# Turning heads, probabilities and gates in 32x32 squares on VectorE, with the squares moved by DMAs within SBUF

## The reference

```python
h = rms_norm(x, norm_w, 1e-6);  proj = h @ w_in        # q_a k/v_c k/v_s k/v_w gates z_a q_b k_b v_b z_b
# group A: 8 heads of 128, 2 kv groups: compressed, selected and window branch, sigmoid gate per head and branch
o_a = g0 * o_cmp + g1 * o_sel + g2 * o_win
# group B: 4 heads with two softmax maps, a = p[:, 0] - lam * p[:, 1]; o = rms_norm(a @ v) * (1 - lambda_init)
mixed = concat([o_a * silu(z_a), o_b * silu(z_b)])
x = x + mixed @ w_out;  return rms_norm(x, final_norm_w, 1e-6)
```

## Time and profile before

| | |
|---|---|
| median of 3 runs | 515.6 us (515.48 to 515.9) |
| profiled execution | 515.5 us |
| its span, first to last instruction | 513.3 us |
| PE, DVE, ACT, POOL busy | 500.3, 282.6, 227.1, 45.2 us |
| data moved by DMA | 107.69 MB, mean 210 GB/s |

### The profile page before, as it was taken

One profiled execution on the slowest core, in us unless ns is written; L12 is line 12 of the kernel. 1 busy time (PEld: TensorE's weight loads), 2 busy tenths in 40 slices (PEclk: granted clock), 3 DMA queues, 4 the chain that ended last, 5 costly groups with the idle time before them and its releaser, 6 DMA issues.

```text
span 513.3 us, 6145 instructions
## 1 busy us (share of the span) xinstructions
PE 500.3 (97%) x2454; PEld 406.0 (79%) x2454; DVE 282.6 (55%) x321; ACT 227.1 (44%) x311; POOL 45.2 (9%) x41
## 2 busy tenths in 40 slices
PE   7999999999999999999999999999999999999993
PEld 6788876667776788888888888888888878888882
DVE  3856813353443957676466647665545544644532
ACT  5847224233232644354644555464544353334231
POOL 1003300010010302010020000001000000113030
PEclk9999999999999999999999999999999999999998
DMA  8998449787778952444343444526864445455004
GB/s 275 412 420 303 163 165 343 282 313 290 305 282 312 348 213 98 165 155 147 109 140 111 160 163 153 185 83 222 332 266 165 170 177 202 189 174 222 14 1 163
DMA packets 17867, 107.69 MB, mean 210 GB/s; under 512 B 2224, under 2 KB 2736, under 8 KB 5936
## 3 DMA queue, kind: packets, MB, share of 16 engines
q1 hardware_dynamic: 16544, 104.86, 54.8%
q10 hardware_dynamic: 1296, 2.44, 1.4%
HBM read 105.20 MB, written 2.10 MB: 209 GB/s over the span
## 4 chain that ended last, share of the span: by engine, by line
PE 93%; issue 2%; DMA 1%; DVE 1%; SPq 1%; ACT 1%; POOLq 0%; POOL 0%; DVEq 0%
PE acc L962 25%; PE acc L964 24%; PE acc L963 24%; PE O L1002 3%; PE S L1104 3%; DMA raw<-stream 1%; PE S L1027 1%; PE S L1121 1%; PE acc L986 1%; PE acc L987 1%; PE acc L988 1%; PE S L1038 1%; PE S L1185 1%; PE S L964 1%; PE S L963 1%
## 5 line engine op out<-in xcount | busy, mean ns | idle before, releaser
L651 DVE TENSOR_TENSOR wlo<-raw,whi 128x2048 fp32r<-128x2048 f32 x72 | 166.4, 2313 | 184.6 <-ACT whi L388 184.4
L388 ACT ACTIVATE whi<-raw 128x2048 fp32r<-128x2048 f32 x72 | 138.1, 1918 | 171.5 <-PE acc L964 107.8
L962 PE MATMUL acc<-whi,hT_hi 128*128 128x512 f32 x432 | 172.6, 399 | 0.9 <-issue 0.9
L964 PE MATMUL acc<-whi,hT_lo 128*128 128x512 f32 x432 | 168.6, 390 | 0.0
L963 PE MATMUL acc<-wlo,hT_hi 128*128 128x512 f32 x432 | 168.3, 390 | 0.0
L962 PEld LDWEIGHTS acc<-whi,hT_hi 128*128 128x128 f32 x432 | 81.1, 188 | 29.4 <-issue 13.6
L964 PEld LDWEIGHTS acc<-whi,hT_lo 128*128 128x128 f32 x432 | 81.1, 188 | 17.4
L963 PEld LDWEIGHTS acc<-wlo,hT_hi 128*128 128x128 f32 x432 | 81.2, 188 | 15.8
L350 POOL TENSOR_TENSOR stage<-stage,stage 128x512 f32<-128x512 f32 (+1 forms) x16 | 25.0, 1574 | 193.1 <-DVE stage L694 193.1
L467 ACT ACTIVATE e<-S,small 128x128 f32<-128x128 f32 (+1 forms) x48 | 19.5, 419 | 26.1 <-DVE small L706 26.1
L962 PE MATMUL acc<-whi,mixA_hi 128*128 128x512 f32 x64 | 25.0, 391 | 0.0
(11 more groups left out here) (160 smaller groups left out, 491.2 us busy)
## 6 DMA issues: line engine op xcount, KB each, us to landing
raw<-stream SPq DMA_DIRECT2D x88, 1024.0 KB, 4.9
raw<-stream SPq DMA_DIRECT2D x6, 512.0 KB, 10.6
x_nat<-x_rows SPq DMA_DIRECT2D x2, 1024.0 KB, 13.1
x_nat<-x_rows SPq DMA_DIRECT2D x1, 2048.0 KB, 7.4
result<-x_nat SPq DMA_DIRECT2D x8, 256.0 KB, 3.2
xTs<-xT SPq DMA_DIRECT2D x3, 512.0 KB, 9.2
raw<-stream SPq DMA_DIRECT2D x4, 256.0 KB, 6.0
fw<-final_w ACTq DMA_DIRECT2D x1, 1024.0 KB, 5.3
```

Source lines behind the costliest of these rows:

```text
L388: act.activation(whi[:, n % SPLIT, :], raw[:, c % RAW, :], ACT.Copy).then_inc(hi_ready, 1)
L651: dve.tensor_tensor(wlo[:, n % SPLIT, :], raw[:, c % RAW, :], whi[:, n % SPLIT, :].bitcast(f32), ALU.subtract)\
L962: pe.matmul(acc_bank(n), xh, wh, start=k == 0, stop=False)
L964: last = pe.matmul(acc_bank(n), xl, wh, start=False, stop=k == KT - 1)
```

## The change

Three kinds of turning leave PE: 8 blocks of heads, 6 units of probabilities, 4 blocks of gates. Each is now done as follows. One or three `dve.transpose` turn every 32x32 square in its place. Then SP issues 16 DMAs, each of which moves 32 partitions of an SBUF tile to another group of 32 partitions of another tile (1 KB a partition for heads and gates, 1.5 or 0.75 KB for probabilities). Everything that needs the block waits for all 16.

`HEADS_AT` becomes 7, 9, 24, 32, 40, 45, 49, 53 for the eight blocks, `Z_AT` is 64, 68, 72, 76 and `MIX_AT` 66, 70, 74, 77. The DMAs stand in SP's queue between the loads: `moves(c - RAW - 2)` comes behind the load of chunk `c`. ACT's `take_heads` is gone; the scale of the queries is in `rope`. Queries lie so that consecutive tokens are 8 elements (32 bytes) apart, keys in runs of 32. The probabilities are turned by DVE in step U + 2, behind the weighting, where PE did it after chunk U + 3; `take_pT` and `take_pT_lo` read SBUF in place of `S`, and stay in step U + 4. The windows of the compression are built in step 9 in place of 8, by six instructions for two.

```diff
-HEADS_AT = {0: 7, 1: 9, 3: 24, 4: 32, 5: 42, 6: 46, 7: 50, 8: 54}
+HEADS_AT = {b: 7 if b == 0 else LAST["in", b] + 2 for b in ROPE}
+Z_AT = {b: LAST["in", b] + 1 for b in Z}
+MIX_AT = {b: LAST["in", b] + (2 if b == 14 else 3) for b in Z}
-        qbT = sb("qbT", [P, 8, SEQ], at=r1)
-        kbT = sb("kbT", [P, 8, SEQ], at=r1 + 8192)
+        qbT = sb("qbT", [P, 2, 4, Q32, TT, 4], at=r1)
+        kbT = sb("kbT", [P, 2, 4, TT, 4, Q32], at=r1 + 8192)
...
+        def queries(m, h, t):
+            return m[:, h // 4, :, :, t, h % 4].rearrange("p i a -> p (i a)")
+        def keys(m, h, tiles):
+            return m[:, h // 4, :, 0:tiles, h % 4, :].rearrange("p i t a -> p t i a")
...
+            def move_heads(b):
+                sp.wait_ge(heads_turned, ROPE.index(b) + 1)
...
+                for j in range(4):
+                    for i in range(4):
+                        d = dst[Q32 * j:Q32 * (j + 1), i] if b else dst[Q32 * j:Q32 * (j + 1), :, i]
+                        sp.dma_start(d, src[Q32 * i:Q32 * (i + 1), j]).then_inc(heads_in[b], 16)
+            def move_probs(u):
+                sp.wait_ge(probs_turned, u + 1)
+                for j in range(4):
+                    for i in range(4):
+                        sp.dma_start(probsT[n][Q32 * j:Q32 * (j + 1), i], blocksP[n][Q32 * i:Q32 * (i + 1), j])\
+                            .then_inc(probs_in[u], 16)
...
             for c in range(RAW, N_CHUNKS):
...
+                moves(c - RAW - 2)
...
             def take_pT(u):
                 if u:
                     act.wait_ge(pv_done, TT * u)
+                act.wait_ge(probs_in[u], 16 * 16)
                 for k in range(3):
-                    act.wait_ge(probs_turned, 3 * u + k + 1)
-                    act.activation(pT[:, k, 0:w], S[:, k, 0:w], ACT.Copy).then_inc(pT_hi_ready, 1)
+                    act.activation(pT[...], probsT[n][:, :, k].rearrange("p i h a -> p h i a"), ACT.Copy)...
...
+            def turn_blocks(dst):
+                return dve.transpose(dst, stage[:, :, :].rearrange("p t (h j a) -> p (t h) j a", h=4, j=4))
+            def turn_heads(b):
+                dve.wait_ge(rope_ready, TT * (n + 1))
+                if n:
+                    dve.wait_ge(heads_in[ROPE[n - 1]], 16 * 16)
+                turn_blocks(...).then_inc(heads_turned, 1)
+            def turn_probs(u):
+                dve.wait_ge(probs_ready, before + TT * n)
+                for k, (t, kt) in enumerate(((0, 0), (1, 0), (1, 1))):
+                    last = dve.transpose(blocksP[n][:, :, k].rearrange("p j h a -> p h j a"),
+                                         e[:, 0:n, kt * P:(kt + 1) * P].rearrange("p h (j a) -> p h j a", j=4))
+                last.then_inc(probs_turned, 1)
...
                     if c == UNIT_AT[u] + 2:
                         (weights if u < N_A else weights_b)(u)
+                        turn_probs(u)
...
-                for b in ROPE:
-                    if c == HEADS_AT[b]:
-                        turn_heads(b)
                 for u in range(N_UNITS):
-                    if c == UNIT_AT[u] + 3:
-                        turn_probs(u)
...
-                for b in range(11, N_IN):
-                    if c == LAST["in", b] + (1 if b == 14 else 2):
-                        turn_z(b)
```

More of the change, by code:

```diff
@@ L289, in _, with move_z, moves @@
                 sp.dma_start(raw[:, c, k * NB:(k + n) * NB], stream[c, :, k * NB:(k + n) * NB]).then_inc(w_in[i], 16)
+            def move_heads(b):
+                sp.wait_ge(heads_turned, ROPE.index(b) + 1)
+                if b == 5:
+                    sp.wait_ge(cmp_out, 1)
+                src, dst = blocks[b], heads(b)
+                for j in range(4):
[3 more added lines that the diff above has]
+            def move_probs(u):
+                n = 4 if u < N_A else 2
+                sp.wait_ge(probs_turned, u + 1)
[3 more added lines that the diff above has]
+                            .then_inc(probs_in[u], 16)
+            def move_z(b):
+                k = b - Z[0]
+                sp.wait_ge(z_turned, k + 1)
+                if k == 0:
+                    sp.wait_ge(scores_done, TT * N_UNITS)
+                if k >= 2:
+                    sp.wait_ge(mix_lo, TT * k)
+                for j in range(4):
+                    for i in range(4):
+                        sp.dma_start(zT[k][Q32 * j:Q32 * (j + 1), i], blocksZ[Q32 * i:Q32 * (i + 1), j])\
+                            .then_inc(z_in[b], 16)
+            def moves(c):
+                for b in ROPE:
+                    if c == HEADS_AT[b]:
+                        move_heads(b)
+                for u in range(N_UNITS):
+                    if c == UNIT_AT[u] + 2:
+                        move_probs(u)
+                for b in Z:
+                    if c == Z_AT[b]:
+                        move_z(b)
             for c in range(RAW, N_CHUNKS):
@@ L428, in take_v @@
                 dst = values(b, t)[0]
+                if b == 9:
+                    act.wait_ge(heads_in[8], 16 * 16)
                 act.activation(dst, a[:, :], ACT.Copy, scale=rstd[:, t:t + 1]).then_inc(acc_read["s"], 1)
[L431 to L439, removed]
             def take_hid(k):
@@ new lines, in turn_z @@
+            def turn_z(b):
+                k = b - Z[0]
+                if k < 2:
+                    dve.wait_ge(acc_read["s"], reads("s", TT * (b + 1)))
+                else:
+                    dve.wait_ge(zb_ready, TT * (k - 1))
+                if k:
+                    dve.wait_ge(z_in[b - 1], 16 * 16)
+                else:
+                    dve.wait_ge(pT_lo_ready, 3 * N_UNITS)
+                turn_blocks(blocksZ[:, :, :, :, :].rearrange("p j t h a -> p (t h) j a")).then_inc(z_turned, 1)
@@ new lines, in turn_probs @@
+            def turn_probs(u):
+                n = 4 if u < N_A else 2
+                before = sum(8 if v < N_A else 4 for v in range(u))
+                dve.wait_ge(probs_ready, before + TT * n)
+                for k, (t, kt) in enumerate(((0, 0), (1, 0), (1, 1))):
+                    e = e0 if t == 0 else e1
+                    last = dve.transpose(blocksP[n][:, :, k].rearrange("p j h a -> p h j a"),
+                                         e[:, 0:n, kt * P:(kt + 1) * P].rearrange("p h (j a) -> p h j a", j=4))
+                last.then_inc(probs_turned, 1)
@@ L934, in _ @@
         def _(pe):
-            turned = {"heads": 0, "units": 0, "pT": 0}
             def products(c, tiles=(0, 1), after_tile=None):
@@ L1006, in products_cmp, with scores_free @@
                 last.then_inc(hid_done if ends(c) else chunk_used, 1)
[L1008 to L1029 removed]
+            def scores_free(u):
+                if u:
+                    pe.wait_ge(exp_done, 8 * u)
             def gate_products():
```

217 lines of the change are left out of this document (100 added, 117 removed).

## The result

The changed kernel takes 575.96 us (median of 4 runs, 573.43 to 581.09) against 515.73 (515.48 to 515.9) on the same chip: ratio 1.118, 95% interval 1.114 to 1.121. The forecast was 523.8, with 505 to 537 as its range. The sign was right, the size was not: +60 us instead of +8. Of all runs reported here one, 530.4 us of the kernel with two queues, was in a slower state of the chip and is left out of that kernel's figures; with it its median is 524.7 instead of 524.25.

A forecast was written before the change was run, and what follows sets the result against it. PE, busy 97% of the span, was taken as the bound. Terms -1.7 - 1.0 - 1.9 + 11.6 - 2.9 + 4.1 = +8.2 us on the 515.6 median gave 523.8 us, range 505 to 537.

The forecast's parts named there:

- 16 DMAs issued in a row: SP's issue of one block's move: 0.40 us for each DMA, bounds 0.37 and 0.50.
- L: Time from a block's last square turned to its last byte landed: 8.2 us, bounds 7.1 and 10.1.
- The mechanism of the units: In attention units PE waits for moved probabilities and later units start their chains late: +11.6 us for units 1 to 5.
- It decides at L = 6.2: Threshold of the rival that moves fit: at most 6 us from turning to landing, no PE waits, about 504 us; chance 0.20.
- 30 to 32: Sign that the forecast is right: starts of scores in the units 30 to 32 us apart; 26.5 would show it wrong.
- I charge nothing: In SP's queue, heads' sixteen issues take 6.4 us and end about when the next squares are turned: no cost.
- Heads, early and in the compression's stage: Heads' transposes leaving PE: -1.7 us for blocks 0 and 1, -1.0 for heads 3 and 4 after 0.7 for delays.
- Gates: Gate transposes leaving PE: 3 x -0.87 us for blocks 11 to 13, -0.3 for block 14, together -2.9.
- Strided weights: PE's stationary queries read 32 bytes apart, loads at 1.6 times the dense price: +4.1 us, bounds 0 and 7.
- The clock: Rival: PE idling before each weighted sum lowers its clock, 13 us more, 537 us in total; chance 0.08.
- the -17.3 of transposes: All transposes leaving PE, heads 7.0, probabilities 6.5, gates 3.8: 17.3 us gained if nothing else were late.
- the -9.1 that the transposes of these units would give: Gain that units 1 to 5 would have from removed transposes alone, against the +11.6 us forecast for them.

The follow-up runs named there:

- the kernel with two queues: The changed kernel with each block's sixteen DMAs issued half by SP and half by GpSimd, at the same time; 524.25 us.
- The probe: A separate kernel computing nothing of the reference, timing DMA issues by form and queue and matmuls with strided stationary operands; SP's copies within SBUF took 0.59 us in a row.
- the dose: Table over six kernels of turned-to-copied time against the time of units 1 to 4; each microsecond above 6.5 in one unit costs 1.3 to 1.6 us.
- with one DMA each: The changed kernel with all 18 blocks moved by one 128-partition DMA instead of sixteen, exchange between partition groups left out; 512.99 us.
- the kernel with only the hidden moves: The kernel before, with only heads 5 to 8 and gates 11 to 13 turned by DVE and moved, heads written into the old dense layout; 509.93 us.

## Why the prediction was wrong

- **The step that failed** is "16 DMAs issued in a row": 0.40 us each, bounds 0.37 and 0.50. It was 0.63, above the upper bound. I had bounded an operation that the trace didn't show, a copy within SBUF, by rows of loads from HBM, and let the small size pull the value down. The probe shows that bytes, and 32 or 64 partitions, do nothing and the kind does. From turned to landed L = 15 x 0.63 + 2.0 = 11.4 us instead of 8.2, and 12.3 until copied (mean of units 1 to 5) with what the queue adds.
- **The mechanism of the units held**, with its threshold: "It decides at L = 6.2", and two queues with 6.5 lose 1.8 us. The size of what lies above was near too: the forecast's own bounds, -5.5 to +9.5 for L from 7.1 to 10.1, are 5.0 us to each microsecond in five units, and the dose has 1.3 a unit. For five units and 12.3 instead of 8.2 that is 5 x 1.3 x 4.1 = 27 us. The scores came 34.5 to 40.1 us apart, where 30 to 32 was to be the sign.
- **"I charge nothing" for moves that meet on SP** failed too, but in small, and follows from the first: sixteen issues of heads take 10.0 us, not "6.4, just over one chunk of 5.5", so the probabilities' stand behind them. With sixteen DMAs for the probabilities, those of the heads make units 1 to 4 3.8 us longer (147.5 against 143.7). This is in the 12.3 already.
- **Heads, early and in the compression's stage**: -1.7 and -1.0 in the forecast, +2.9 and +9.5 in the trace; with one DMA each they are -1.7 and -0.1. Early, PE waits 3.8 us for the windows that DVE builds, where I had allowed for 2.5 at most. In the compression's stage each move of 10.0 us makes the loads behind it late, and ACT's splits with them (below). The cover, "some 20 us", was that of the units' loads. I had seen that less is free here and put 0.7.

```profile
144.45 1.91 ACT L464 ACTIVATE whi<-raw 128x2048 fp32r<-128x2048 f32 x1 [8.27 <-DMA raw<-stream]
...
175.06 1.91 ACT L464 ACTIVATE whi<-raw 128x2048 fp32r<-128x2048 f32 x1 [8.82 <-DMA raw<-stream]
```

- **Gates**: 11 to 13 as forecast (the kernel with only the hidden moves has their gain). Block 14 was put at -0.3 and is -1.3 + 9.3 = +8.0 in the two last rows of the stages. PE waits 6.4 us for its subtraction, since 16 issues end 10.0 us after they begin, and the granted clock is at 1.2 GHz for 6.8 us behind the wait.
- **Strided weights**: +4.1, upper bound 7. The load is 2.1 times the dense one at 2.4 GHz, not 1.6 (0.225 against 0.106; 16 against the compressed keys take some 3.5 us, where 2.7 was to be the sign), and the clock adds to it: 14.1 where nothing hides it, 7.6 in the changed kernel. My upper bound had set the load's price right at twice, but counted no clock.
- **The clock**, a rival at 0.08, did come: the digits below 9 between 200 and 360 us that were to be its sign are there (0.87 and 0.90 in the windows of the units). It comes behind the waits and the strided loads and doesn't replace them as the cause: with one DMA to a block, PE waits for no probabilities and the windows of the units are at full clock but for two falls in unit 0. Its own price in the changed kernel stays open. A mean of 0.945 over 575.1 us is some 63 us at 1.2 GHz, so by an estimate at most 32 us, a part of them in stretches where PE would have waited anyway.
- **Right**: that SP's issues outweigh the landing of a copy of 48 KB (10.0 against 2.0 us); that PE's waits are ended by DVE's `pT_lo` and ACT waits at `take_pT`; the -17.3 of transposes (with one DMA to a block and dense weights the kernel is at 498.91, 17.2 below the one before); DVE's prices. The Trainium skill's rule (DMA: Bandwidth & Descriptors, "Issuing engines are not separate DMA queues") that initiating is small beside the DMA didn't hold for these copies: 10.0 us of issues against 2.0 of landing. What it says of several engines, that they save the time to initiate, did: 576 to 524.25.
- **A slip**: "the -9.1 that the transposes of these units would give" should be -7.8 (3 x 0.87 + 3 x 1.31 + 2 x 0.65). Nothing is added up from it.

By stage, in the two profiled executions, the forecast of +8.2 missed the +61.8 by 53.6 us. The heads ahead of the compression are 4.6 of it, the compression's stage 10.5, block 14 8.3, and the units 30.2 (+36.3 and +5.1 against the 11.6 and 4.1 less 1.9 and 2.6). Of the 30.2, L is about 27 and the strided weights 7.6 - 4.1 = 3.5. With one DMA to a block 63.0 us are gone, so all of these but the strided weights go back to the sixteen issues, by the waits and the late loads behind them. It is an account after the fact, with a slope read from the same runs, and not a forecast.

## What to carry to other kernels

Before a step is cut into many small DMAs, measure the issue of exactly that kind of DMA on exactly that queue, and multiply: a serial price of 0.6 us times sixteen was 10.0 us here, beside a landing of 2.0. Then ask of each move what waits for it and what stands behind it in the queue; the same sixteen DMAs cost 0 us where nothing does (heads 5 to 8, gates 11 to 13) and 8 us where one engine waits (gate 14). Other engines' work of some 6 us hid the move in a unit; only the part above that counted, and it counted again in each unit but the first. And a probe needs its own check: look at the granted clock of each of its groups before you compare them.

## What the runs showed of the hardware

- A copy of 32 partitions within SBUF costs the issuing engine 0.59 us on SP, 0.61 on ACT and 0.50 on GpSimd in a row, on SP the same for 64 bytes, 1 KB and 4 KB to a partition and for 64 partitions (0.60); with HBM on one side 0.42 on SP.
- GpSimd ends with a drain of 11.52 us in the kernels that issue 128 or more DMAs from its queue, 2.21 in the probe with four, and 1.04 without any; 4.9 us of the 11.52 show in the span.
- A stationary operand at a stride of 32 bytes costs 0.225 us to a load in the kernels on average (gaps of 0.238 at either level of the clock), in place of 0.106 dense at 2.4 GHz. At 1.2 GHz the probe has 0.213 dense and 0.21 to 0.24 for strides of 8 to 64 bytes.
- The granted clock fell to 1.2 GHz with PE busy without a gap in the records, in runs of matmuls with 16 columns: with dense loads in the probe, with strided ones in the kernel with one DMA to a block.
- A copy within SBUF of 768 KB in one DMA landed 3.5 us after its issue, and 7.9 us when a load of 1 MB was issued 0.57 us ahead of it.
- Writing in runs of 128 bytes instead of 1 KB cost SP's issue 0.02 us more and left the landing at 1.9 us (1.8 for the same heads in runs of 1 KB).
